# The mixture of experts sums, norms and writes out its result rows expert by expert, instead of in a pass at the end

## The reference

```python
h = rmsnorm(x1, norm_ffn_g)
for e in range(N_EXPERTS):                      # 32, two of them per row with weight != 0
    hid = silu(h @ w_gate[e]) * (h @ w_up[e])   # 1024 -> 256
    y = y + combine[:, e:e + 1] * (hid @ w_down[e])
y_out = rmsnorm(x1 + y, final_norm_g)
```

## Time and profile before

| | |
|---|---|
| median of 3 runs | 795.87 us |
| profiled execution: its time, its span | 795.66 us, 793.8 us |
| expert stage: first gather, first gate matmul, last gate, last down matmul | 416.9, 431.1, 747.0, 753.5 us |
| behind the last matmul | 40.3 us |
| busy share of PE, DVE, ACT, POOL | 91%, 69%, 52%, 14% |
| DMA in the expert stage | 0.92 to 0.96 busy, 352 to 368 GB/s |

### The profile page before, as it was taken

How to read it: one execution, slowest core, us unless ns; L and a number is a source line. 1 busy time by engine, 2 the same in 40 slices (tenths; PEclk the granted TensorE clock), 3 DMA queues, 4 the chain that set the end, 5 groups by cost and what they waited for, 6 DMA issues and landing times.

```text
span 793.8 us, 11743 instructions
## 1 busy us (share of the span) xinstructions
PE 718.5 (91%) x3793; PEld 559.6 (70%) x3793; DVE 545.9 (69%) x932; ACT 411.4 (52%) x659; POOL 113.6 (14%) x154
## 2 busy tenths in 40 slices
PE   5899999999999889999986999999999999999900
PEld 3577887877877668888875677777777777777600
DVE  4755855765777773435774788888888777777767
ACT  6444454445357432212123777777777666777523
POOL 1010110010011010000002222222222222210153
PEclk9999999999999999999987999999999999999955
DMA  8950710011032436224185599999999999996647
GB/s 337 338 159 5 182 54 26 26 53 39 14 107 100 175 113 260 79 80 167 46 338 233 223 339 365 379 359 361 377 368 367 363 355 354 358 359 255 265 166 284
DMA packets 46393, 175.21 MB, mean 221 GB/s; under 512 B 12032, under 2 KB 16072, under 8 KB 34072
## 3 DMA queue, kind: packets, MB, share of 16 engines
q1 hardware_dynamic: 37144, 157.86, 53.8%
q0 software_dynamic: 9216, 16.93, 5.6%
HBM read 156.03 MB, written 35.37 MB: 241 GB/s over the span
## 4 chain that ended last, share of the span: by engine, by line
PE 79%; DMA 10%; DVE 5%; issue 2%; ACT 1%; POOL 0%; SPq 0%; POOLq 0%; DVEq 0%; ACTq 0%
PE psZ L806 20%; PE psZ L1135 14%; PE psZ L973 12%; PE psS L1166 9%; DMA wg<-w_up 6%; PE psT L737 6%; PE psZ L1139 6%; PE psS L841 2%; PE psO L867 2%; PE psG L1019 2%; DMA xg<-h_d,ic_src 1%; PE psT L1007 1%; DMA y_d<-y_t,ic_dst 1%; PE psO L780 1%; PE psG L876 1%
## 5 line engine op out<-in xcount | busy, mean ns | idle before, releaser
L2129 DVE TENSOR_TENSOR wg_lo<-wg,wg_hi 128x1024 fp32r<-128x1024 f32 x96 | 114.2, 1216 | 14.3 <-ACT wg_hi L1253 14.1
L1253 ACT ACTIVATE wg_hi<-wg 128x1024 fp32r<-128x1024 f32 x96 | 98.6, 1059 | 39.3 <-DMA wg<-w_up 23.2
L806 PE MATMUL psZ<-wi_hi,xT_hi 128*128 128x512 f32 (+1 forms) x256 | 96.7, 378 | 3.3 <-DVE wi_lo L1612 3.3
L2139 DVE TENSOR_TENSOR wd_lo<-wd,wd_hi 128x2048 fp32r<-128x2048 f32 x31 | 72.1, 2326 | 39.3 <-ACT wd_hi L1253 39.3
L806 PE MATMUL psZ<-wi_lo,xT_hi 128*128 128x512 f32 (+1 forms) x256 | 93.7, 366 | 0.0
L806 PE MATMUL psZ<-wi_hi,xT_lo 128*128 128x512 f32 (+1 forms) x256 | 93.7, 366 | 0.0
L1135 PE MATMUL psZ<-wg_hi,xg_hi 128*128 128x512 f32 x192 | 78.3, 408 | 4.7 <-DVE xg_nat L2122 2.8
L1135 PE MATMUL psZ<-wg_hi,xg_lo 128*128 128x512 f32 x192 | 75.9, 395 | 0.0
L1135 PE MATMUL psZ<-wg_lo,xg_hi 128*128 128x512 f32 x192 | 75.9, 395 | 0.0
L2316 POOL DMA_INDIRECT y_d<-y_t,ic_dst x32 | 37.9, 1184 | 244.0 <-DVE ic_src L2101 151.9
L806 PEld LDWEIGHTS psZ<-wi_hi,xT_hi 128*128 128x128 f32 x256 | 48.0, 188 | 19.8 <-issue 12.1
(11 more groups left out here) (277 smaller groups left out, 1388.4 us busy)
## 6 DMA issues: line engine op xcount, KB each, us to landing
wg<-w_gate SPq DMA_DIRECT2D x32, 1024.0 KB, 9.8
wg<-w_up SPq DMA_DIRECT2D x32, 1024.0 KB, 21.3
wd<-w_down SPq DMA_DIRECT2D x32, 1024.0 KB, 16.0
x_t<-x_rows SPq DMA_DIRECT2D x9, 512.0 KB, 3.4
y_d<-wo_stage SPq DMA_DIRECT2D x1, 4608.0 KB
mix_d<-mix_t SPq DMA_DIRECT2D x9, 512.0 KB, 2.7
m_t<-mix_d SPq DMA_DIRECT2D x9, 512.0 KB, 3.6
h_d<-h_t SPq DMA_DIRECT2D x9, 512.0 KB, 2.6
```

The source lines that it names most:

```text
L806: last = nc.tensor.matmul(psZ[g % 2][:, 0:n], a[:, c, :], w[g // 2][:, c, w0:w0 + n], start=(k == 0), stop=(k == 3 * DC - 1))
L1253: return nc.scalar.activation(out, in_, ACT.Copy)
L2129: tt(wg_lo[k][:, :, c, :], wg[k][:, :, c, :], wg_hi[p][:].bitcast(F32), ALU.subtract).then_inc(s_wgl, 1)
L2139: tt(wd_lo[k][:], wd[k][:], wd_hi[:].bitcast(F32), ALU.subtract).then_inc(s_wdl, 1)
```

## The change

- x1 is no longer kept. Each tile goes from a ring of 4 (`x1r`) to two DRAM tensors: `s_d`, whose rows have 1,024 sums and then the row's two result weights (`ROW` = 1,026), and `x1_d`, for the overflow branch alone. The weights are stored to `s_d` in one DMA of 8-byte pieces.
- Each expert gathers its rows of `s_d` into `xb` (3 buffers): `gather_base`. DVE adds weight times result, straight from PSUM: `sum_y`, which takes the place of ACT's `y_out`. Rows for which the expert is the lower one are scattered back to `s_d` (`scatter_lower`, experts 0 to 27, after the second weight was copied over the first). For experts 4 to 31 ACT squares (`square_y`), POOL takes the power (`row_factor`), DVE scales (`scale_y`), and the rows for which it is the upper one are scattered to the output (`scatter_upper`). `gather_base(e)` waits until `scatter_lower(e-3)` has landed.
- The index table has three columns per expert: source, lower, upper. The copies of single index columns (L2101, L2107) go.
- `N_SPLIT` is 4: four chunks are split, four are float32. The pieces `wg_hi` have 4 buffers.
- The zeros of `y_d`, the reading back and the whole pass at the end go. Weights of expert 1 are loaded in tile 6 of stage 2, those of expert 2 after the last output matmul, those of expert 3 when the first gather has landed (before: 1, 2 and 3 in a row from 398.5 us). The loops over experts are written out.

```diff
-N_SPLIT = 6
+N_SPLIT = 4
 N_PIECE = N_SPLIT // 2
+ROW = D + 2
...
+            def store_x1(t):
+                sp.wait_ge(s_x1, 2 * t + 2)
+                sp.dma_start(rows(s_d, t)[:, 0:D], x1(t)).then_inc(s_xst[t % 2], 16)
+                sp.dma_start(rows(x1_d, t), x1(t)).then_inc(s_xst[t % 2], 16)
...
             sp.wait_ge(s_op, 2 * T)
-            load_expert(1)
+            load_expert(2)
             store_h(T_P)
-            load_expert(2)
+            x1_read(5)
+            sp.dma_start(fing[:], fin_g.to_broadcast([P, D])).then_inc(s_gain, 16)
+            sp.wait_ge(s_rv, 7)
+            sp.dma_start(s_d.rearrange("(t p) n -> p t n", p=P)[:, :, D:ROW], w_of[:]).then_inc(s_wst, 16)
+            sp.wait_ge(s_ga[0], 16)
             load_expert(3)
...
+            def square_y(e):
+                act.wait_ge(s_ya, e + 1)
+                j, b = 2 * (e - NGRP), e % 2
+                if j > 2:
+                    act.wait_ge(s_fr, e - NGRP - 1)
+                nc.scalar.activation(junk3[:], xb[e % 3][:, 0:D], ACT.Square, scale=D ** -0.5,
+                                     accum_out=small[:, 40 + 4 * b:41 + 4 * b]).then_inc(s_fsq, 1)
...
+            def sum_y(e):
+                dve.wait_ge(s_dn, e + 1)
+                base_ = xb[e % 3]
+                dve.wait_ge(s_gb[e % 3], (e // 3 + 1) * 16)
+                if e < NE - 1:
+                    last = stt(out=base_[:, 0:D], in0=psS[:], scalar=base_[:, D:D + 1], in1=base_[:, 0:D], op0=ALU.mult,
+                               op1=ALU.add)
...
+            def scale_y(e):
+                n, b = e - NGRP, e % 2
+                dve.wait_ge(s_fr, n + 1)
...
+                stt(out=y_t[b][:], in0=xb[e % 3][:, 0:D], scalar=small[:, 42 + 4 * b:43 + 4 * b], in1=fing[:], op0=ALU.mult,
+                    op1=ALU.mult).then_inc(s_fo, 1)
...
+            def gather_base(e):
+                if e > 2:
+                    pool.wait_ge(s_scl, 16 * (min(e - 3, NE - NGRP - 1) + 1))
+                if e > NGRP + 2:
+                    pool.wait_ge(s_fo, e - 3 - NGRP + 1)
+                settle(pool)
+                take(idx[:, e], xb[e % 3], s_d, s_gb[e % 3])
...
+            def stage4(e):
+                if e + 5 < NE:
+                    gather_h(e + 5)
+                if e > NGRP + 1:
+                    scatter_upper(e - 2)
+                if e + 1 < NE:
+                    gather_base(e + 1)
+                if 0 < e <= NE - NGRP:
+                    scatter_lower(e - 1)
+                if e > NGRP:
+                    row_factor(e - 1)
```

More of the change, by code:

```diff
@@ L278, in build @@
         y_t = [s4.take(f"y_t{b}", [P, D], F32) for b in range(2)]
-        wg_hi = [s3.take(f"wg_hi{b}", [P, 2, 2, FE], F32R) for b in range(2)]
+        wg_hi = [s3.take("wg_hi0", [P, 2, 2, FE], F32R), Region(nc, base, a1, at4).take("wg_hi1", [P, 2, 2, FE], F32R)]
         sg = s4.take("sg", [P, FE], F32)
@@ L450, in build @@
         o_done = sem("o_done")
-        s_yy = [sem(f"s_yy{b}") for b in range(4)]
-        s_ysum = sem("s_ysum")
         s_fsq = sem("s_fsq")
@@ L1207, in _ @@
             keep_busy(7)
-            for k in range(4):
-                stage4(k, k)
-            with pe.Fori(4, NE - 7, 4) as e:
-                for k in range(4):
-                    stage4(e + k, k)
-            for k in range(4):
-                stage4(NE - 4 + k, k)
+            for e in range(NE):
+                stage4(e, e % 4)
             pe.wait_ge(s_dTh, NE)
@@ L2323, in gather4 @@
                 settle(pool)
[L2324 to L2333 removed]
+                take(idx[:, e], xg[e % 4], h_d, s_ga[e % 4])
+            def gather_base(e):
[3 more added lines that the diff above has]
+                    pool.wait_ge(s_fo, e - 3 - NGRP + 1)
+                settle(pool)
+                take(idx[:, e], xb[e % 3], s_d, s_gb[e % 3])
@@ L2340, in _ @@
-            gather4(4, 0)
-            for k in range(4):
-                stage4(k, k)
-            with pool.Fori(4, NE - 11, 4) as e:
-                for k in range(4):
-                    stage4(e + k, k)
-            for e in range(NE - 8, NE):
-                stage4(e, e % 4)
+            for e in range(5):
+                gather_h(e)
+            for b in range(2):
+                pool.wait_ge(s_xst[b], 32 * ((T - b + 1) // 2))
+            pool.wait_ge(s_wst, 16)
+            gather_base(0)
@@ L2348, in _ @@
+            for e in range(NE):
+                stage4(e)
+            scatter_upper(NE - 2)
+            row_factor(NE - 1)
+            scatter_upper(NE - 1)
             most = pool.value_load(cnt_i[0:1, :], min_val=0, max_val=N_TOK)
             for b in range(2):
-                pool.wait_ge(s_sc4[b], NE // 2 * 16)
+                pool.wait_ge(s_scu[b], (NE - NGRP) // 2 * 16)
             with pool.If(most > SLOTS):
-                with pool.Fori(0, (N_CHUNK - 1) * NE) as n:
+                with pool.Fori(0, N_CHUNK * NE) as n:
@@ L2358, in _ @@
                     settle(pool)
-                    gather(0, o_ga)
+                    take(ic, xg[0], h_d, o_ga)
                     pool.wait_ge(o_ya, 2 * n + 2)
                     settle(pool)
-                    scatter(0, o_sc)
-                    pool.wait_ge(o_sc, 16 * n + 16)
+                    for k in range(2):
+                        put(ic, 1 + k, y_d[k], y_t[0], o_sc)
+                    pool.wait_ge(o_sc, 32 * n + 32)
+                for t in range(T):
+                    n = N_SAMPLE if t == T_P else P
+                    pool.wait_ge(s_fsq, 2 * (NE - NGRP + t) + 2)
+                    ptt(small[0:n, 42:43], small[0:n, 41:42], small[0:n, 1:2], ALU.pow).then_inc(s_fr, 1)
             pool.sem_inc(o_done, 1)
-            for i in range(T):
-                n = final_tile(i)[1]
-                pool.wait_ge(s_fsq, 2 * i + 2)
-                ptt(fst[0:n, i, 2:3], fst[0:n, i, 1:2], small[0:n, 1:2], ALU.pow).then_inc(s_fr, 1)
 def shape_constants():
```

412 lines of the change are left out of this document (177 added, 235 removed).

## The result

| | before | changed |
|---|---|---|
| median | 793.25 us (4 runs) | 843.53 us (4 runs, 842.66 to 846.06) |
| ratio, 95% interval | | 1.064, 1.057 to 1.070 |
| profiled span | 793.8 us | 840.7 us |
| first gather issued, its landing | 416.92, 9.21 us | 424.72, 13.10 us |
| end of the first gate, end of the last | 437.45, 747.0 us | 449.6, 821.4 us |

What follows compares the result with a forecast made beforehand. PE was taken to bind the expert stage first, DMA later. First gate's end 432.2, seven periods at 10.1, 21 at 11.9, three at 11.1, then 6.5, 10.0 and 1.9 gave 804.5, rounded to 805 us; range 780 to 828.

Steps and rivals of the forecast that it cites:

- first to last gate, 31 periods: Expert stage: seven periods at 10.1 us, 21 at 11.9, the last three, without lower scatters, at 11.1.
- The rest I take at nothing: Stage 2 and the zeros: x1's extra 1 MB of stores per tile costs 0, bounds 0 and +3 us.
- I take 4.1: Start of the expert stage: the first gather lands in 4.1 us instead of 9.21, so -5.1.
- the new wait: POOL's loop: scatter landing 10.0, pause 0.30, gather issue 1.02, pause 0.30, DVE's delay 0.3; period 11.9 us.
- seven periods at 10.1 while the lead lasts and landings are short: Early expert stage: PE's period of 10.1 us holds for seven periods while weights loaded ahead hide the DMA, reaching 502.9.
- 13.3: POOL's loop period in us if DVE's two-input instructions and POOL's SBUF reads exclude each other for a whole instruction.
- Bytes alone: Rival, expert stage: scatters land early enough, only bandwidth counts; 785 us at 11.1 a period, 774 at 10.6; 25%.
- Uneven DMA engines: Rival, expert stage: gathers' filled slots load half the 16 DMA engines; period 11.8, 804.5 us, or 11.5 and 797; 20%.
- The loop at its long end: Rival, POOL's loop: landing 11.2 plus up to 1.7 for DVE; period 13.1 to 14.5, 830 us with 13.1; 15%.
- The clock: Rival, PE: its clock falls in gaps of some 2 us a period, a few us slower; 3%.
- PE +0.33: PE's work per expert: 6.21 us for 5.88 with 12 split matmuls and four float32 chunks; period becomes 10.1.
- The end: Behind the last matmul: 10.0 us instead of 40.3, including 0.3 + 3.3 for pause and scatter to landing; upper bound 15.4.

Runs made afterwards that it cites:

- e3: Changed kernel with expert 1's weights loaded behind the last output matmul instead of in tile 6 of stage 2: 836.3 us.
- e2: Changed kernel with the store of the result weights in 8-byte pieces issued only after the first gather has landed: 836.6 us.
- e1: Changed kernel with each stage's lower scatter of e-1 issued on POOL before the gather of sums of e+1, not behind it: 818.6 us.
- e14: Changed kernel with 4 KB weight packets, lower scatter and row factor before the gather of sums, result weights stored after the first gather, expert 1's weights after stage 2: 797.9 us.
- e9: Changed kernel with indirect DMAs taking 96 slots per expert instead of 128, from the fourth use of each buffer on: 846.6 us.
- e18: e14 with indirect DMAs taking 96 slots instead of 128: 827.0 us.
- e5: Kernel before with one part of the change alone, `N_SPLIT` 4, so four chunks of gate and up are plain float32 matmuls: 799.5 us.
- e7: e14 with weights in packets of 8 KB instead of 4 KB: 808.2 us.

## Why the prediction was wrong

The direction was the likeliest of the three, and the place was right: POOL's gather of sums waits for a lower scatter's landing in every period, `scale_y` for the row factor. The size was off by 38.1 us of span (802.6 forecast, 840.7 measured), mostly from three of its steps:

| step | forecast | measured | off by |
|---|---|---|---|
| end of the first gate | 432.2 | 449.6 | +17.4 |
| first to last gate, 31 periods | 353.9 | 371.8 | +17.9 |
| last gate to last matmul | 6.5 | 6.5 | 0 |
| behind it | 10.0 | 12.9 | +2.9 |

**1. "The rest I take at nothing": stage 2.** The forecast counted 1 MB of stores per tile and bounded them by 3 us. It did not count that expert 1's 3 MB, which the change list has in tile 6, go out ahead of the next tiles' inputs. SP's issues:

```profile
367.17 1.16 SPq L608 DMA_DIRECT2D wg<-w_gate  x1
368.37 1.20 SPq L608 DMA_DIRECT2D wg<-w_up  x1
369.62 0.48 SPq L613 DMA_DIRECT2D wd<-w_down  x1
372.60 0.33 SPq L574 DMA_DIRECT2D m_t<-mix_d  x1
```

ACT got that tile at 382.34, after 7.86 us of waiting for it, and PE ran dry:

```profile
382.34 1.06 ACT L1234 ACTIVATE mT_hi<-m_t 128x1024 fp32r<-128x1024 f32 x1 [7.86 <-DMA m_t<-mix_d]
```

```profile
385.00:390.00 5.00, 3.30 (x22) 2.65 (x20) 4.45 (x21) 0.22 (x1) 0.00 (x0) 0.93 0.21 70
390.00:395.00 5.00, 2.83 (x16) 2.54 (x17) 3.27 (x15) 1.36 (x3) 0.38 (x2) 0.50 0.00 0
```

PE lost 3.9 us, fell to a granted clock of 0.50, and the tile's matmuls behind it took 6.80 for 5.46 (393.55 to 400.34). The first gather came 7.8 us late. e3, which puts these loads behind the last output matmul, shows the cause: its first gather is issued 7 us sooner.

**2. "I take 4.1" for the first gather's landing.** It took 13.10: +9.0. The forecast was right that few weights are in flight by then, and dismissed the 8-byte pieces, which are issued 0.8 us behind the gather, as "not needed" until later. Whether they are needed soon was not the question; they share the DMA engines, which were busy while hardly any bytes moved (the issue, then two windows):

```profile
425.51 0.37 SPq L678 DMA_DIRECT2D s_d<-w_of  x1
```

```profile
425.00:430.00 5.00, 1.27 (x12) 1.08 (x10) 2.72 (x6) 0.00 (x0) 4.08 (x4) 1.00 0.81 52
430.00:435.00 5.00, 0.00 (x0) 0.00 (x0) 0.00 (x0) 0.00 (x0) 0.09 (x1) 0.53 0.43 23
```

e2, which only moves this line, gives 4.46. So the forecast's value was right for a kernel without them. Steps 1 and 2 with 0.6 of small changes make the 17.4. Undone one at a time, they gave 7 us each in the whole time.

**3. "10.0 + 0.30 + 1.02 + 0.30 + 0.3 = 11.9 us" for the new wait.** The mechanism was right, the terms too small: a period of the loop is 12.74. Of this 0.84, 0.43 is the landing (10.43 for 10.0) and 0.4 the way from a landing to the next scatter (2.31 for 1.92). The wait costs POOL 0.9 from the landing (607.96) to the gather's issue (608.84), where I had taken the 0.30 of a pause without a wait: I had read it from a row that waited for nothing. The 0.3 for DVE was not needed at the scatter; the gather's issue took 0.12 more than 1.02 instead. Over the 21 periods of the forecast 0.84 makes 17.6 of the 17.9.

Also wrong, but without weight in the number, was "seven periods at 10.1 while the lead lasts and landings are short". The lead of weights is no lead for this loop, which begins with the first scatter at 465 us: its first four landings took 10.88, 11.62, 11.43 and 11.59, longer than later ones. PE ran its first seven periods in 69.1 us and then took 21.4 for one. The loop had 25 turns and not 21; the other periods were that much shorter, so that all but 21 x 12.74 of the 371.8 came to 104.3 for 104.0. That was luck.

The Trainium skill, SBUF — State Buffer, on the shared port, gave 13.3 by my reckoning, nearer to 12.74 than 11.9 is, but not for its reason: the 28 lower scatters' issues took 1.10 us on average, with a median of 1.02, so DVE hardly delayed them. In e1 the scatters are issued as DVE's two-input pass runs, and there the rule shows, 2.18 us for 1.02 (the median of its 28 is 2.19):

```profile
599.00 2.18 POOL L2260 DMA_INDIRECT s_d<-xb,idx  x1 [0.35 <-issue]
```

```profile
598.03 2.29 DVE L2096 TENSOR_TENSOR wd_lo<-wd,wd_hi 128x2048 fp32r<-128x2048 f32 x1
```

**The rivals.** *Bytes alone* was forecast at 785 with 11.1 a period (774 with 10.6). e14 is that case, made by hand, and gives 797.9 with 11.30 over the last 20: the rate fell to 349 GB/s, under the 353 that I had as the lower end. Of the 12.9 between, 3.7 lies before the first gate's end, 5.9 in the 31 periods and 2.9 behind the last matmul. *Uneven DMA engines*: that a gather's filled slots fall on half of the engines fits the steps of the landings. For the gathers of h in the changed kernel the eighth step comes at 6.6 us on average, the ninth at 8.3, the last at 10.5; in e9, with 96 slots, at 9.1, 9.8 and 11.1, with less of a gap (15 gathers each). But the more even spread gained nothing, neither in e9 nor in e18, so the uneven one was not the bound there. (By its own split the rival should have counted 33 KB and not 17 KB of scatter per engine, which gives 11.7 for 11.8.) *The loop at its long end* came nearest (830 at 15%), but its reasons, a landing of 11.2 and a pass of DVE before the issue, were not there. The clock fell in the gaps (0.90 to 0.97), which I had at 3%; that its cost lies inside the measured waits, since PE is not the bound, is argued and not tested. *PE +0.33*: e5 bears it out, with 10.08 for 10.1.

**The end** was right in kind: 12.9 for 10.0, at most 15.4. Behind the last scaling the scatter was issued at 834.81, 1.15 us later and not 0.3, and the span ended 5.9 us behind that issue, where I had 4.4.

## What to carry to other kernels

A wait for a DMA's landing that closes a circle (landing, issue, landing) sets the period by latency, and idle engines and a DMA share that falls are its signature; price the landing under the kernel's own load, from its first turn on. Turning the order opened the circle and let the queue behind it fill up: ask what the next late thing is before counting the gain. Small stores issued next to an urgent gather, and loads issued ahead of the next tile's input, cost what they share, not when they are needed.

## What the runs showed of the hardware

- The landing of an indirect DMA depended on the packet size of the hardware queue beside it: 10.35 us with 8 KB packets, 8.74 and 8.95 with 4 KB, 7.1 with 2 KB; 4.46 for the first gather of e2, beside DMA engines that are 0.20 busy (420 to 425 us). Empty slots did not count (10.38 with 96 slots, 10.47 with one more empty DMA).
- Indirect DMAs of one queue land one behind another: before, a gather 3.7 us behind the scatter that was issued 1.3 us ahead of it. In e1, with four issued within 6 us beside 8 KB packets, all kinds become late, the gathers of h with 16.2 us for 10.5, the lower scatters in the chain with 18.1; with 4 KB packets (e14) the lower scatters land in 8.4, in a kernel that differs from e7 (17.8 in the chain) in the packets alone. The Trainium skill, DMA: Bandwidth & Descriptors, in the section on queues, rings and completion order, says that each DMA engine takes turns between queues and drains a packet of some 9 to 17 descriptors from one before it goes to the next.
